# Mixer B's queries and keys laid feature by feature: transposes replaced by DMA, low halves moved to GpSimd, seven taps to VectorE

## The reference, cut to what matters

```
qb = (rms_norm(cq) @ w_uq).reshape(B, S, 8, 64 + 32)      # 384 -> 8 heads x (64 nope + 32 rope)
q_nope, q_rope = split(qb, [64]);  q_rope = apply_rope(q_rope)
kvb = (rms_norm(ckv) @ w_ukv).reshape(B, S, 8, 64 + 64)   # 256 -> 8 heads x (64 key + 64 value)
k_nope, v_b = split(kvb, [64]);    k_rope = apply_rope(kr)  # one rotary key for all heads
q_full = concat(q_nope, q_rope);   k_full = concat(k_nope, k_rope)
y_b = causal softmax attention(q_full, k_full, v_b)
```

## Time and profile before

| what | value |
|---|---|
| median of 3 runs | 1781.49 us |
| span of the profiled execution | 1779.5 us (the runs lie 2.0 us above it) |
| PE busy | 1755.8 us, 99% |
| DVE busy | 1289.0 us, 72% |
| ACT busy | 966.7 us, 54% |
| POOL busy | 816.9 us, 46% |
| start of attention in layer 0 | 156.6 us |

### The profile page before, as it was taken

The page is one execution under the profiler, slowest core; times in us unless marked ns, Lnnn a source line. Parts: engine busy times, 40 slices in busy tenths (PEclk is TensorE's granted clock), DMA queues, the critical chain, the costliest instruction groups (busy, mean ns, idle before and its releaser), DMA issues.

```text
span 1779.5 us, 29532 instructions
## 1 busy us (share of the span) xinstructions
PE 1755.8 (99%) x10254; PEld 1547.5 (87%) x10254; DVE 1289.0 (72%) x2503; ACT 966.7 (54%) x1905; POOL 816.9 (46%) x464
## 2 busy tenths in 40 slices
PE   9999999999999999999999999999999999999997
PEld 9888888878889999988898888888787899999886
DVE  6279988867799888713363899887778998887033
ACT  4544777844476565622244557787444665555222
POOL 5446942354434333354434569434444333344542
PEclk9999999999999999999999999999999999999999
DMA  6322121123332323233333322111233333322331
GB/s 192 99 94 93 60 60 60 60 71 101 101 119 96 119 96 106 85 118 107 95 98 102 100 84 60 60 60 60 83 104 98 103 112 100 116 96 95 119 98 68
DMA packets 47082, 166.69 MB, mean 94 GB/s; under 512 B 5472, under 2 KB 5728, under 8 KB 46944
## 3 DMA queue, kind: packets, MB, share of 16 engines
q1 hardware_dynamic: 46080, 163.60, 28.8%
q10 hardware_dynamic: 864, 1.28, 0.3%
HBM read 162.76 MB, written 2.10 MB: 93 GB/s over the span
## 4 chain that ended last, share of the span: by engine, by line
PE 65%; DVE 4%; ACT 1%; issue 1%; POOL 0%; DMA 0%; DVEq 0%; ACTq 0%; SPq 0%; POOLq 0%
PE banks L1163 18%; PE banks L1165 18%; PE banks L1164 18%; PE banks L1215 2%; PE banks L1217 2%; PE banks L1216 2%; PE banks L1271 1%; PE banks L1318 1%; DVE sb_u L1869 0%; DVE sb_xl L1876 0%; DVE banks L1711 0%; DVE sb_u L1839 0%; PE banks L1377 0%; PE banks L1302 0%; PE banks L1247 0%
## 5 line engine op out<-in xcount | busy, mean ns | idle before, releaser
L624 POOL TENSOR_TENSOR sb_wl<-sb_wraw,sb_wh 128x1024 fp32r<-128x1024 f32 x205 | 499.9, 2442 | 614.8 <-ACT sb_wh L752 589.0
L1163 PE MATMUL banks<-sb_xh,sb_wh 128*128 128x512 f32 (+1 forms) x1152 | 405.7, 352 | 1.9 <-ACT sb_h_qa L923 0.8
L1165 PE MATMUL banks<-sb_xh,sb_wl 128*128 128x512 f32 (+1 forms) x1152 | 389.2, 338 | 0.0
L1164 PE MATMUL banks<-sb_xl,sb_wh 128*128 128x512 f32 (+1 forms) x1152 | 388.5, 337 | 0.0
L752 ACT ACTIVATE sb_wh<-sb_wraw 128x1024 fp32r<-128x1024 f32 x199 | 210.4, 1058 | 266.2 <-PE banks L1165 171.4
L1165 PEld LDWEIGHTS banks<-sb_xh,sb_wl 128*128 128x128 f32 x1152 | 218.7, 190 | 24.2
L1163 PEld LDWEIGHTS banks<-sb_xh,sb_wh 128*128 128x128 f32 x1152 | 219.3, 190 | 22.8 <-issue 3.7
L1164 PEld LDWEIGHTS banks<-sb_xl,sb_wh 128*128 128x128 f32 x1152 | 219.6, 191 | 13.6
L1163 PE MATMUL banks<-sb_t_hi,sb_wh 128*128 128x256 f32 x768 | 217.5, 283 | 3.6 <-DVE banks L2141 3.6
L1164 PE MATMUL banks<-sb_t_lo,sb_wh 128*128 128x256 f32 x768 | 217.3, 283 | 0.0
L1165 PE MATMUL banks<-sb_t_hi,sb_wl 128*128 128x256 f32 x768 | 217.3, 283 | 0.0
(11 more groups left out here) (348 smaller groups left out, 4051.8 us busy)
## 6 DMA issues: line engine op xcount, KB each, us to landing
sb_wraw<-in_weights SPq DMA_DIRECT2D x256, 512.0 KB, 3.5
sb_wraw2a<-in_weights SPq DMA_DIRECT2D x24, 512.0 KB, 3.6
sb_wraw2b<-in_weights SPq DMA_DIRECT2D x24, 512.0 KB, 4.5
sb_u<-in_x SPq DMA_DIRECT2D x8, 256.0 KB, 6.6
out<-sb_u SPq DMA_DIRECT2D x8, 256.0 KB, 2.1
sb_praw<-in_ple ACTq DMA_DIRECT2D x2, 512.0 KB, 4.3
sb_par<-in_params ACTq DMA_DIRECT2D x2, 98.5 KB, 2.9
sb_rope_tmp<-in_freq ACTq DMA_DIRECT2D x1, 24.0 KB, 4.4
```

Of the source, the lines that this page charges most:

```text
L624: nc.gpsimd.tensor_tensor(wl[:, t % WS, :], wraw[:, t % 2, :], wh[:, t % WS, :].bitcast(F32), ALU.subtract).then_inc(lo_ready, 1)
L1163: nc.tensor.matmul(out, wh_, xh_, start=start, stop=False, skip_group_check=onto)
L1164: nc.tensor.matmul(out, wh_, xl_, start=False, stop=False, skip_group_check=onto)
L1165: return nc.tensor.matmul(out, wl_, xh_, start=False, stop=stop, skip_group_check=onto)
```

## The change

The groups are cut anew: "uqr" (rotary part of all heads' queries, 256 columns), "uqn" (the other part, 512), "uk" (keys, 512), "uv" (values, 512). For "uqn" and "uk" the weights are the stationary operand and the tokens the moving one, so that the result has features as rows: `qn_t` and `kn_t` hold two heads in each block of 128 rows. The rotary part is still made token by token, turned by DVE, and then transposed at once for all heads by 8 transposes before tile T_GATE-2 ("rope queries") into `qr_t`.

The rows of head h are laid at rows 0 to 95 of `q_raw` and 0 to 63 of `k_raw` by three DMAs on SP (`load_head`), issued at fixed places between the weight loads. `q_raw` and `k_raw` share the memory of `q_l` and `k_l`: head h can be loaded once the scores of head h-2 are done. ACT makes the high halves from there; the low halves are made by POOL for heads 1 to 7 (semaphore `b_low`, which PE's score 4h waits for) and by DVE for head 0. POOL keeps 7 taps, and DVE gets 7 more: a second one in slots 1, 5, 9, 13, 28, 43 and 58. POOL's accumulator and product move to `th_conv`.

```diff
+FEATURE_GROUPS = ("uqn", "uk")
-POOL_TAPS = 14
-POOL_TAPS_AT = {T_GATE + LEAD + n: range(2 * n, 2 * n + 2) for n in range(POOL_TAPS // 2)}
+POOL_TAPS = 7
+POOL_TAPS_AT = {T_GATE + LEAD + n: range(n, n + 1) for n in range(POOL_TAPS)}
+HEAD_LOW_AT = {T_GATE + LEAD + n: h for h, n in enumerate((1, 2, 4, 5, 6, 8, 9), 1)}
...
+HEAD_AT = {T_GATE + 2: (0, 1), T_GATE + 6: (2,), T_GATE + 8: (3,), T_GATE + 9: (4,), T_GATE + 10: (5,),
+           T_GATE + 12: (6,), T_GATE + 13: (7,)}
...
-FRONT += [("tile", t) for t in range(T_U, T_GATE)]
+FRONT += [("tile", t) for t in range(T_U, T_GATE - 2)] + [("rope queries", 0)]
+FRONT += [("tile", t) for t in range(T_GATE - 2, T_GATE)]
...
+            def load_head(layer, h):
+                if h == 0:
+                    sp.wait_ge(scored, layer * 12 + 12)
+                    sp.wait_ge(qr_out, layer * 2 + 2)
+                    sp.wait_ge(group_out, layer * OUTS + (OUTS - NT))
+                elif h >= 2:
+                    sp.wait_ge(score_ready, layer * UNITS + head_free(h))
+                half, quarter = slice(BN * (h % 2), BN * (h % 2) + BN), slice(BR * (h % 4), BR * (h % 4) + BR)
+                sp.dma_start(q_raw[0:BN, h % 2], qn_t[half, h // 2]).then_inc(q_loaded[h % 2], 16)
+                sp.dma_start(q_raw[BN:BQ, h % 2], qr_t[quarter, h // 4]).then_inc(q_loaded[h % 2], 16)
+                sp.dma_start(k_raw[0:BN, h % 2], kn_t[half, h // 2]).then_inc(k_loaded[h % 2], 16)
...
+                for t in range(*HEAD_TILES):
+                    load(t % 2, first + t)
+                    for h in HEAD_AT.get(t, ()):
+                        load_head(layer, h)
...
                     for k in POOL_TAPS_AT.get(t, ()):
                         tap(layer, k)
+                    if t in HEAD_LOW_AT:
+                        h = HEAD_LOW_AT[t]
+                        pool.wait_ge(b_high, layer * 2 * BH + (2 * h + 2))
+                        nc.gpsimd.tensor_tensor(q_l[0:BQ, h % 2], q_raw[0:BQ, h % 2], q_h[0:BQ, h % 2].bitcast(F32),
+                                                ALU.subtract).then_inc(b_low, 1)
+                        nc.gpsimd.tensor_tensor(k_l[0:BN, h % 2], k_raw[0:BN, h % 2], k_h[0:BN, h % 2].bitcast(F32),
+                                                ALU.subtract).then_inc(b_low, 1)
...
+                        act.wait_ge(q_loaded[n % 2], 32 * (layer * BH // 2 + n // 2 + 1))
+                        nc.scalar.activation(q_h[0:BQ, n % 2, :], q_raw[0:BQ, n % 2, :], ACT.Copy).then_inc(b_high, 1)
...
+            def turn_rope_queries(layer):
+                pe.wait_ge(roped_u, layer * 2 + 2)
+                pe.wait_ge(group_out, layer * OUTS + (OUTS - NT))
+                for c in range(2):
+                    for b in range(NT):
+                        last = nc.tensor.transpose(psum[:, 2 + c, b * P:b * P + P], uqr[:, b, c * P:c * P + P], ident[:])
+                last.then_inc(qr_turned, 1)
...
                     if qt == 0:
-                        pe.wait_ge(qk_low, layer * LOWS + (LOW_AT[ready_at(n)] + 1))
+                        if hd == 0:
+                            pe.wait_ge(qk_low, layer * LOWS + (LOW_AT[("rope", 0)] + 1))
+                            pe.wait_ge(b_first, layer * 2 + 2)
+                        elif hd < BH:
+                            pe.wait_ge(b_low, (layer * (BH - 1) + hd) * 2)
...
-                    v.tensor_tensor(lo[0:rows, n % 2, :], psum[0:rows, bank, :], hi[0:rows, n % 2, :].bitcast(F32),
-                                    ALU.subtract).then_inc(qk_low, 1)
+                    v.tensor_tensor(lo[0:rows, 0, :], raw[0:rows, 0, :], hi[0:rows, 0, :].bitcast(F32),
+                                    ALU.subtract).then_inc(b_first, 1)
```

More of the change, by code:

```diff
@@ L142 @@
 for _slot in range(UNITS):
-    _n = 1 if _slot <= KEEP_SLOT or (_slot - KEEP_SLOT) % 15 == 14 else 2
+    _n = 1 if _slot <= KEEP_SLOT and (_slot not in PREP or PREP[_slot][0] != "B") else 2
     TAPS_AT.append(TAPS[_taps:_taps + _n])
@@ L723, in logit @@
             return NT - 1 - k // IH, k % IH
[L726 removed]
+        tile_group, t = {}, 0
         for g, (name, ncol, nk, tiles) in enumerate(TOKEN_GROUPS):
[L728 removed]
             for k in range(tiles):
@@ L903, in _ @@
                         continue
+                    if kind == "rope queries":
+                        act.wait_ge(qr_turned, layer + 1)
+                        for c in range(2):
+                            nc.scalar.activation(qr_t[:, c], psum[:, 2 + c, :], ACT.Copy).then_inc(qr_out, 1)
+                        continue
                     if kind == "tile":
@@ L1264, in bank_for, with turn_blocks @@
                             pe.wait_ge(value_out, layer * HEADS + (before[1] + 1))
-                    return BANK_AT[(kind, n, part)]
-                def turn_blocks(kind, n, part, blocks, rows):
-                    bank = bank_for(kind, n, part)
+                    return BANK_AT[(kind, n)]
+                def turn_blocks(kind, n, blocks, rows):
+                    bank = bank_for(kind, n)
                     for b, src in enumerate(blocks):
@@ L1423, in _ @@
                         scratch(n, layer)
+                    elif kind == "rope queries":
+                        turn_rope_queries(layer)
                     elif n in tile_group:
@@ L1724, in lows @@
                     mixer, n = which
-                    part = "k" if kind == "prep keys" else "q" if mixer == "B" else ""
-                    bank = BANK_AT[("prep", which, part)]
-                    dve.wait_ge(turn_out, turns + (TURN_AT[("prep", which, part)] + 1))
                     if mixer == "A":
+                        bank = BANK_AT[("prep", which)]
+                        dve.wait_ge(turn_out, turns + (TURN_AT[("prep", which)] + 1))
                         v.tensor_tensor(q_h[AD:P, n % 2, :], psum[0:AD, bank, :], q_h[0:AD, n % 2, :].bitcast(F32),
@@ L1770, in attention @@
                         select(step, back=0)
-                    if slot in PREP and PREP[slot][0] == "B":
-                        lows("prep keys", PREP[slot])
                 steps.end("V_ATTN", V_ATTN)
```

159 lines of the change are left out of this document (89 added, 70 removed).

## The result

The changed kernel takes 1787.57 us (median of 7 runs, 1785.27 to 1791.97) against 1781.65 us of the kernel before (7 runs, 1781.07 to 1784.33): a ratio of 1.0034, 95% interval 1.0024 to 1.0043. It is slower, by 5.9 us, and outside the predicted range of 1771.5 to 1785.5. The profiled execution is the slowest of the seven. Their times go with the mean clock that TensorE was granted: 1785.3 and 1785.7 at 0.996, 1786.9 and 1787.6 at 0.995, 1788.5 at 0.994, 1789.6 at 0.993, 1792.0 at 0.992.

What follows compares the result with a forecast made beforehand. PE bounds the kernel, busy 1755.8 of 1779.5 us. Per layer -5.6 - 1.45 + 1.6 + 3.0 + 0.5 = -1.95, for two layers -3.9: span 1775.6, plus 2.0 gives 1777.6 us; range 1771.5 to 1785.5.

Steps and rivals of the forecast that it cites:

- Transposes that go: PE in attention: 14 blocks of four transposes fewer per layer at 0.40 us each, saving 5.6 us per layer.
- Bank stops that go: Slots 6, 10 and 14: PE's transposes no longer wait for DVE's low halves of queries, saving 1.45 us per layer.
- Projections: PE's projection matmuls are cut anew with the same columns: nothing, within 0.3 us either way.
- Rotary queries: Before attention: PE waits for DVE's rotation 48 matmuls earlier than before, costing 1.6 us per layer with the hand-over.
- GpSimd's low halves of head 1: Score 4: PE waits for POOL's low halves from 174.9 to 177.9, costing 3.0 us per layer.
- What that stop does to the clock: Behind the stop at head 1: a slower PE clock, counted as nothing in the sum and left to rival 3.
- rival 3: Behind head 1's stop: the clock falls to 1.2 GHz, 5.5 us more per tile, 1788.6 with both layers; 12%.
- Heads 2 to 7: Later heads in attention: POOL's low halves about even at head 3, nothing elsewhere, costing 0.5 us per layer.
- DVE and POOL: DVE's load falls, POOL's is no lighter and is now waited for; nothing on PE from DVE's exchange.
- DMAs: Head rows loaded on SP's queue, critical at heads 3 and 6: counted 0, at most 2 us twice a layer.
- Rival 2: Start of attention: DVE's low halves of head 0 and POOL's tile T_GATE+3 collide, 1781.8 to 1784.8 us; 15%.
- Rival 4: Heads 3 and 6: ACT stands for late DMAs and PE's turns behind it, 1779.6 to 1784.6 us; 10%.

Runs made afterwards that it cites:

- e2b: Changed kernel with 15 multiplications of constants on TensorE in front of head 1's wait, filling that stop: 1783.41 us, ratio to the kernel before 1.0007.
- e13: Changed kernel with the low half of head 0's values made by GpSimd before its weight tile instead of by VectorE: 1782.57 us, ratio 1.0004.
- e14: Changed kernel with only the rows of heads 3 and 6 issued one weight tile earlier: 1787.24 us, ratio 1.0025.
- e8: e1 with the rows of heads 3 and 6 issued one weight tile earlier: 1778.63 us, ratio to the kernel before 0.9980.
- e10: e9 with the rotary queries turned one weight tile later in the front: 1772.86 us, ratio to the kernel before 0.9951.
- e9: e8 with the low half of head 0's values made later, in slot 3, still on VectorE: 1775.91 us, ratio 0.9967.
- e11: e8 with rotary queries one tile later and the low half of head 0's values on GpSimd ahead of tile T_GATE+3: 1772.19 us, ratio 0.9950.
- e6: Kernel before with only 7 taps moved from GpSimd to VectorE: 1788.09 us, ratio 1.0031.
- e1: Changed kernel with a head's two low halves on GpSimd placed before the same tile's tap: 1796.04 us, ratio to the kernel before 1.0078.

## Why the prediction was wrong, step by step

The sum forecast -1.95 us a layer; layer 0 shows +4.06 at score 31. The 6.0 us between them lie at the start (0.7), at scores 1 to 3 (0.9), in head 1's stop (0.8), in the clock behind it (2.6) and behind score 8 (1.0, of which the late rows of head 6 are 0.6; the rest was not traced). In the medians the forecast of 1777.6 was missed by 10.0 us: the clock is 4.2 of them (e2b), and the terms of 0.7, 0.9, 0.8 and 0.6 us a layer make 6.0. So the clock is the largest term that was missing, and not the only one: e2b, without it, is still 5.8 us above the forecast.

The steps that failed are the clock, put at 0, and the chain to head 1's low halves, which left out VectorE's collision with GpSimd. They are not independent: the collision makes the stop longer and the stop costs the clock, so filling the stop (e2b, 4.2 us) and taking away the collision (e13, 5.0 us) each bring the kernel level with the one before. In the order of the prediction:

- **Transposes that go** (5.6 a layer): right. 0.74 to 0.88 us a head against 2 x 0.40.
- **Bank stops that go** (1.45): right that they go, wrong that nothing comes in their place. Stops for VectorE's low halves of the probabilities (L1395) are 0.85 us a layer, against 0.25 in the kernel before; the 0.6 between them go with e14. In e8, where TensorE comes earlier, they are 1.55.
- **Projections** (0): nothing in the scores speaks against it; not measured by itself.
- **Rotary queries** (+1.6): right; 1.4 idle, and 2.0 at the scores when e10 takes it away. Score 0 is 2.2 later and not 1.5, within the scatter of that column.
- **GpSimd's low halves of head 1** (+3.0): the chain was the right one and 0.8 too short. VectorE's collision at the values' low half (2.61 us, 0.92 in the kernel before) is 1.7 of the 2.45 us by which the first mask is later than its 168.0; the stops at scores 2 and 3 go with it in e9, e11 and e13.
- **What that stop does to the clock** (0 in the sum): the larger of the steps that failed. The prediction held that a stop of 3.0 us was "longer than any of these" and priced the fall, but put it beside the sum as rival 3 with 12%. It happened in both layers: 2.64 and 2.94 us, half of the 5.5 that rival 3 named. In e14 the same stop cost 2.5 us in layer 0 and 1.5 in layer 1, where the slow clock lasted half as long, so the price differs from execution to execution. Without it (e2b) the kernel is level with the one before. The row that the prediction read for a clock of 1.00 could not show a fall behind its stop either: its window ends at 529.00 and the stop at 529.79. That profile has no fall there, but the changed kernel's has (534).
- **Heads 2 to 7** (+0.5): 0.6 for head 3. Right.
- **DVE and POOL** (0): nothing in TensorE's waits speaks against it for the changed kernel, as e14 has no more stops at L1395 than the kernel before. It is true only while VectorE's slots have room: e6 shows 2.7 us a layer where its low halves stay, and the faster kernels e8 and e11 have stops of 1.55 us a layer at that line, against 0.25 before.
- **DMAs** (0): 0.6 us a layer at head 6 (e14), within the 2 us allowed, and so little only thanks to the stop ahead of them (e1, e8).

Of the rivals, 3 came true in mechanism and, at 1788.6, nearly in time; the time was near because its clock term was too large and its sum too small. Rival 2 was right that the two engines collide, and its sign came (a low half of over 2 us on VectorE at the start of attention); it was wrong on the instruction: head 0's two low halves took 0.69 and 0.68 us, the values' low half next to them 2.61. Rival 4 waited behind both and showed at head 6 alone.

The collision was priced as a slowdown copied from one row. The rows of the last section show something else: VectorE's instruction, where it comes second, stands until GpSimd's tile has ended, so the price is what is left of a tile of 2.40 us. The rows of before fit that too: in rows 9 and 7 the tile ends at 142.11 + 3.87 = 145.98 and line 1587 at 143.75 + 2.77 = 146.52. The Trainium skill says so in "SBUF — State Buffer", section "SBUF: two separate sides": the pair of ports is held for a whole instruction by whichever starts first, and not shared. By that rule the values' low half, 0.05 us behind the tile, takes the 2.34 us that are left of it and its own 0.41, 2.75 in all; the trace agrees nearly, with 2.61. GpSimd's taps do not fit the rule (last section), and there the measurement decides.

## What to carry to other kernels

A stop of TensorE has two prices, the wait and the clock behind it. A forecast stop longer than any in the trace must carry the second price in the sum. The clock can also fall behind a stop that cost nothing in another execution, so compare profiles by stretch, and take out the falls that the change did not bring. When a wait is taken away, look for what it has hidden: removing 3.8 us at head 1 made this kernel 8.5 us slower until two DMAs were issued one tile earlier.
